# Hybrid decoder step on one core: joint level products, a readout in four quarters, and sample outer products in 32-row groups

## Chip, core and metric

The kernel runs on one core of one Trainium2 chip. The metric is the device time of one execution in microseconds (us).

## What is computed

The reference is one layer of a decoder for 256 prompt tokens and 8 sample tokens (each sample token belongs to a sequence of its own, with a stored state). The layer has two token mixers of eight heads each, a gated merge and a feed-forward block:

```python
proj = rms_norm(x, norm_mix) @ w_in            # q,k,v,gate (retention); query,forget,input,gate (HGRN2); merge gates
o_r, s_ret_new = retention_chunkwise(q, k, v, s_ret, log_gamma)     # state per head: 128 x 256
o_h, s_hg_new = hgrn2_chunkwise(qh, k_in, logf, i, s_hg)            # state per head: 128 x 128
#   for one sample token:  S = decay * S + k^T v ;  o = S^T q
x = x + (sigmoid(ga) * (o_r @ w_ret_out) + sigmoid(gb) * (o_h @ w_hgrn_out)) @ w_out
x = x + SwiGLU(rms_norm(x, norm_ffn)) ;  y = rms_norm(x, norm_final)
```

All inputs and outputs are fp32; the outputs include the new states of the prompt and of the eight samples.

## The kernel before

Tokens lie along the free dimension: 256 prompt columns and 8 sample columns, 264 in all (`T`). Weights are streamed from memory in chunks of 512 KB (four blocks of 128 rows by 256 columns). Each chunk passes through four engines in a fixed order: SyncE's queue (SP) loads it into `raw`; ScalarE (ACT) rounds it to fp32r into `hi` (L426); VectorE (DVE) writes the rest, `raw - hi`, into `lo` (L723); TensorE (PE) does 24 matmuls with it (`use_chunk`, L1082 to L1084: `hi` with the high part of the activations, `hi` with the low part, `lo` with the high part). Each of the three buffers is a ring of four, so an engine works at most four chunks ahead of the next.

The first stage is a loop over eight heads, 20 chunks a head: four for the HGRN2 query and forget logits, four for retention q and k, four for v, four for the HGRN2 input and gate, four for the retention gate. All engines run their own hand-written program in order. Between the chunks stands the work of the mixers: after chunk i of a head PE calls `tail(i)`, which finishes the head before, and `attend(i)`, which works on this head; ACT and DVE have the matching steps in the same places, after the chunk that they prepare four ahead. PSUM has two pairs of banks for the chunks (`pA`, `pB`) and four banks for the mixers: `p4`, `p56` (two banks) and `p7`. Counters such as `p4_full` and `p4_free` hand each bank from PE to its reader and back, in a numbered order of uses per head (`SC0`, `OR1`, ...).

The steps that the change touches:

- `tail(0)`: PE turns the 16 x 384 readout `o16` of the last head to columns (L1124, L1126); DVE adds the two parts of each sample.
- `attend(11)` and `attend(13)`: transposes of keys and values for both prompt blocks (L1103), and of the samples' keys and values (`rows_of`, L1107), which DVE had split into a high and a low fp32r part (L774, L776). DVE then spreads the keys over eight masked copies (`k_only`, L799).
- `attend(14)` and `attend(15)`: the outer products k^T v of the samples, four samples at a time, each a 32-row matmul (L1113) into both banks of `p56`; DVE adds each four to the decayed state `S_ret` (L905). Beside them the prompt's new state (L1164) and the prompt's outputs (L1170, L1172).
- `attend(16)`: within-block scores of HGRN2 by seven levels. GpSimd (POOL) prepares for each level a masked key `k_lev` and a query `q_lev` (L668 to L691). PE multiplies them for prompt block 0 (L1194) and for block 1 (L1196), seven matmuls each, into overlapping places of `p56`; DVE picks what it needs with seven predicated copies (L934), after a product with the identity (L917) and copies (L920, L924).
- `attend(17)`: eight outer products of the samples for HGRN2 (L1203); DVE updates `S_hg` (L941).
- `attend(19)`: the readout o = S^T q of all samples. ACT and DVE first split both new states into fp32r parts (L524, L532, L544, L809). For each sample PE multiplies both parts with a weight of 16 columns, in which only this sample's query (two parts) is not zero (`q_only`, `hq_only`, L793), and adds all up in 16 rows of `p7` (L1224).

The state of a head is loaded on SP between the chunks 13 and 14 (L371, L373), once the last head's has been written back (ACT's queue, L552, L554).

Of the kernel before, what the change touches and what calls it, by code (L numbers as in the profile page):

```python
# [41 lines left out]
P = 128  # L42
# [5 lines left out]
H = 8  # L48
# [39 lines left out]
K_IDENT = K_LEVEL + NLEV * 64  # L88
K_KDEC = K_IDENT + P
K_GAMMA = K_KDEC + 2 * H  # L90
K_EYE8 = K_GAMMA + H
K_ROW8 = K_EYE8 + NS * NS
K_SIZE = K_ROW8 + NS
# [13 lines left out]
def build(nc, consts, vectors, xT, w_in, w_ret, w_hg, w_out, w_fin, w_fout, s_ret, s_hg,  # L107
          yT, ret_p, hg_p, ret_s, hg_s):
    with ExitStack() as ctx:
# [35 lines left out]
        lb_tmp = alloc(heads, "lb_tmp", [P, 4, H])  # L145
        norm_tmp = ExitStack()
# [5 lines left out]
        hkey = alloc(heads, "hkey", [P, T])  # L152
        hquery = alloc(heads, "hquery", [P, T])
# [9 lines left out]
        v_rows = alloc(heads, "v_rows", [8 * NS, RV], F32R)  # L163
# [3 lines left out]
        key_pair = alloc(heads, "key_pair", [P, 2, 4, NS], F32R)  # L167
        k_parts, hk_parts = key_pair[:, 0], key_pair[:, 1]
        v_parts = alloc(heads, "v_parts", [P, 3, 4, NS], F32R)
        k_only = alloc(heads, "k_only", [8 * NS, NS, DK], F32R)  # L170
        q_parts = alloc(heads, "q_parts", [P, NS, 2], F32R)
        hq_parts = alloc(heads, "hq_parts", [P, NS, 2], F32R)

        q_only = alloc(heads, "q_only", [P, NS, 2, NS], F32R)
        hq_only = alloc(heads, "hq_only", [P, NS, 2, NS], F32R)
        o16 = alloc(heads, "o16", [2 * NS, 384])
# [8 lines left out]
        k_lev = [alloc(heads, f"k_lev{i}", [P, NP]) for i in range(NLEV)]  # L185
# [17 lines left out]
        S_ret_hi = alloc(heads, "S_ret_hi", [P, NS, RV], F32R)  # L203
        S_ret_lo = alloc(heads, "S_ret_lo", [P, NS, RV], F32R)
        S_hg_hi = alloc(heads, "S_hg_hi", [P, NS, HV], F32R)
        S_hg_lo = alloc(heads, "S_hg_lo", [P, NS, HV], F32R)
# [32 lines left out]
        c_level = cst[:, K_LEVEL:K_LEVEL + NLEV * 64].bitcast(I32).rearrange("p (l j) -> p l j", l=NLEV)  # L239
        c_kdec = cst[:, K_KDEC:K_KDEC + 2 * H].rearrange("p (b h) -> p b h", b=2)  # L240
        c_eye8 = cst[:, K_EYE8:K_EYE8 + NS * NS].rearrange("p (b j) -> p b j", b=NS)
        c_row8 = cst[0:8 * NS, K_ROW8:K_ROW8 + NS]
# [40 lines left out]
        hg_sig_done = sem("hg_sig_done")  # L283
        products = sem("products")
# [6 lines left out]
        state_hi = sem("state_hi")  # L291
        state_split = sem("state_split")
# [120 lines left out]
        def _(act):  # L413
# [46 lines left out]
            def tail(i, h):  # L460

                if i == 0:
                    act.wait_ge(sample_outputs, h * 2)
                    fn(o_sq[:, 0:2, :], oT[:], ACT.Square).then_inc(outputs_squared, 1)
                    fn(o_sq[:, 2, :], ohT[:], ACT.Square).then_inc(outputs_squared, 1)
                elif i == 2:
                    act.wait_ge(p56_full, h * N56 + (SS5 + 1 - N56))
                    fn(o_inv[:, 0, :], p56[:, 0, 0:T], ACT.Sqrt, bias=epsilon[:], scale=1.0 / RV)
                    fn(o_inv[:, 1, :], p56[:, 1, 0:T], ACT.Sqrt, bias=epsilon[:], scale=1.0 / HV
                       ).then_inc(p56_free, 1)  # L470

            def head(h, first=False):
# [3 lines left out]
                for i in range(HEAD_CHUNKS):  # L476
# [25 lines left out]
                    elif i == 13:  # L502
# [3 lines left out]
                        copy(v_rows[0:4 * NS], p56[0:4 * NS, 1, 0:256]).then_inc(p56_free, 1)  # L506
                    elif i == 14:

                        act.wait_ge(p7_full, h * N7 + (SF1 + 1))
                        act.wait_ge(prompt_out_ret, h * 16 + 16)  # L510
                        copy(ret_stage[:], p7[:, 0, 0:RV]).then_inc(p7_free, 1)
                        act.wait_ge(p7_free, h * N7 + (SF1 + 2))
                        act.dma_start(ret_p[bass.ds(h, 1)].rearrange("h d e -> (h d) e"), ret_stage[:]
                                      ).then_inc(prompt_out_ret, 16)
                    elif i == 15:

                        act.wait_ge(b_free, h * 2 + 3)
                        fn(hg_sig[:], hig[:, 1, :], ACT.Sigmoid).then_inc(hg_sig_done, 1)

                        act.wait_ge(normed, h * 4 + 4)  # L520
                        act.wait_ge(p4_full, h * N4 + (OR1 + 1))
                        copy(oT[:, :, 0:NP], p4[:, 0, :].rearrange("p (e n) -> p e n", e=2)).then_inc(p4_free, 1)
                        act.wait_ge(p56_free, h * N56 + (OUT1 + 2))
                        copy(S_ret_hi[:, 0:4, :], S_ret[:, 0:4, :]).then_inc(state_hi, 1)  # L524
                    elif i == 16:

                        act.wait_ge(p7_full, h * N7 + (TI2 + 1))
# [3 lines left out]
                        act.wait_ge(p56_free, h * N56 + (OUT1 + 3))  # L531
                        copy(S_ret_hi[:, 4:8, :], S_ret[:, 4:8, :]).then_inc(state_hi, 1)  # L532
                    elif i == 18:

                        act.wait_ge(p4_full, h * N4 + (OH3 + 1))
# [3 lines left out]
                        act.wait_ge(p4_free, h * N4 + (OH3 + 2))  # L539
# [3 lines left out]
                        act.wait_ge(p56_free, h * N56 + (OUTH4 + 2))  # L543
                        copy(S_hg_hi[:], S_hg[:]).then_inc(state_hi, 1)  # L544
                    elif i == 19:
# [4 lines left out]

                        act.wait_ge(state_split, h * 3 + 3)
# [4 lines left out]

                        act.wait_ge(p7_full, h * N7 + (RD3 + 1))
                        copy(o16[:], p7[0:2 * NS, 0, 0:384]).then_inc(p7_free, 1)
# [65 lines left out]
        def _(pool):  # L624
            tt = nc.gpsimd.tensor_tensor
            pool.sem_inc(normed, 4)

# [15 lines left out]
            for i in range(NLEV):  # L643
                nc.gpsimd.memset(k_lev[i][:], 0.0).then_inc(products, 1)

            steps = 2 + 4 * NLEV + 4
# [10 lines left out]
            def levels(h):  # L657

                count = [NLEV]
# [13 lines left out]
                for i in range(NLEV):  # L673
# [6 lines left out]
                    shape = [P, NP // (2 * s), s]  # L680
# [3 lines left out]
                    step(tt(kl0, k0, g0, ALU.mult))  # L684
# [6 lines left out]
                step(tt(kbar, hkey[:, 0:NP], run_g[:], ALU.mult))  # L691
                assert count[0] == NLEV + steps
# [22 lines left out]
        def _(dve):  # L715
# [56 lines left out]
            def parts(hi_out, lo_out, x, h, n):  # L772

                nc.vector.tensor_copy(hi_out, x).then_inc(parts_done, 1)  # L774
                dve.wait_ge(parts_done, h * 14 + (2 * n + 1))
                tt(lo_out, x, hi_out.bitcast(F32), ALU.subtract).then_inc(parts_done, 1)  # L776

            def twice(x):
                return x.rearrange("p (a b) -> p a b", a=1).broadcast_to([P, 2, NS])

            def key_parts(out, x, h, n):
                parts(out[:, 0:2, :], out[:, 2:4, :], twice(x), h, n)

            def value_parts(out, x, h, n):
                parts(out[:, 0:4:2, :], out[:, 1:4:2, :], twice(x), h, n)

            def query_parts(out, x, h, n):
                parts(out[:, :, 0], out[:, :, 1], x, h, n)

            def masked_query(out, q):  # L790

                shape = [P, NS, 2, NS]
                tt(out, q.bitcast(F32).rearrange("p b (c a) -> p b c a", a=1).broadcast_to(shape),  # L793
                   c_eye8.rearrange("p b (a j) -> p b a j", a=1).broadcast_to(shape), ALU.mult).then_inc(masked, 1)

            def masked_keys(out, rows64):

                shape = [8 * NS, NS, DK]
                return tt(out, rows64.rearrange("p (a d) -> p a d", a=1).broadcast_to(shape),  # L799
                          c_row8.rearrange("p (b a) -> p b a", a=1).broadcast_to(shape), ALU.mult  # L800
                          ).then_inc(masked, 1)

            def level_psum(n):

                return bass.AP(tensor=p56, offset=64 * n, ap=[[2 * 512, P], [512 + 64, 2], [1, 64]])

# [576 lines left out]
```

## Time and profile before

| | us |
|---|---|
| median of 3 runs (lowest, highest) | 1834.14 (1831.59, 1836.6) |
| the profiled execution, its own time | 1834.16 |
| span of its trace, first to last instruction | 1832.3 |
| granted TensorE clock, share of full | 0.995 |

The page of the profile gives the busy share of each engine, then the span in 40 equal slices. The first fourteen slices are the loop over the heads. TensorE is at nine tenths or more from the second slice on. VectorE is at seven or eight tenths in the loop and at five to six after it. The 16 DMA engines are at five to seven tenths, 182 GB/s on average. In the trace's lines a matmul's own duration reaches from its start to the modelled end of its pipeline, so matmuls overlap; the time that one costs is read from start to start.

### The profile page before, as it was taken

Reading aid. Unit: us, or ns where it says so; the run is one execution under the profiler, and the core shown is the slowest. Engines: PE = TensorE matmul, PEld = TensorE weight load, DVE = VectorE, ACT = ScalarE, POOL = GpSimd, SP = SyncE. Lnnn points to the kernel's source line nnn. Section 1 sums busy time; section 2 is a strip of 40 time slices with the busy share of each in tenths; the row PEclk is TensorE's granted clock in tenths of the full one; section 3 lists DMA queues with packets and bytes.
Section 4 is the critical chain, followed back from the end, with each engine's and each line's share of the span. In section 5 each row is a group of like instructions: output and inputs, shape, how many; then the busy total and the mean of one; then the engine's idle time right before and its main releaser. Section 6 shows DMA issues by size and latency. Waiting matters only on the chain.

```text
span 1832.3 us, 37809 instructions
## 1 busy us (share of the span) xinstructions
PE 1785.3 (97%) x14672; PEld 1766.0 (96%) x14672; DVE 1147.5 (63%) x1293; ACT 776.9 (42%) x894; POOL 277.4 (15%) x332
## 2 busy tenths in 40 slices
PE   5999999999999999999999999999999999999997
PEld 5999999999999999999999999999999999999996
DVE  8776877778777675555556665555555555545444
ACT  5454544445444454344444444444444444333332
POOL 4442614416144110000000000000000000000001
PEclk9999999999999999999999999999999999999998
DMA  7665646666466555555547665555565565555552
GB/s 230 192 202 177 197 139 197 190 183 196 140 193 191 184 163 185 184 183 183 182 153 245 192 183 183 182 180 181 181 182 182 183 182 182 185 184 177 179 182 102
DMA packets 388538, 333.86 MB, mean 182 GB/s; under 512 B 11776, under 2 KB 386560, under 8 KB 388352
## 3 DMA queue, kind: packets, MB, share of 16 engines
q1 hardware_dynamic: 369536, 318.88, 56.3%
q10 hardware_dynamic: 18944, 14.16, 2.5%
q8 instruction: 43, 0.70, 0.2%
q14 instruction: 15, 0.12, 0.0%
HBM read 316.67 MB, written 16.32 MB: 182 GB/s over the span
## 4 chain that ended last, share of the span: by engine, by line
PE 82%; DVE 7%; issue 4%; DMA 3%; SPq 2%; ACT 1%; DVEq 0%; POOL 0%; ACTq 0%
PE pA L1082 13%; PE pA L1084 12%; PE pA L1083 12%; PE pB L1082 10%; PE pB L1084 10%; PE pB L1083 10%; PE p L1082 3%; PE p L1084 3%; PE p L1083 3%; DMA raw<-in_w_in 2%; DVE lo L723 2%; PE p L1224 1%; SPq L348 1%; DVE hg_scores L934 1%; SPq L373 1%
## 5 line engine op out<-in xcount | busy, mean ns | idle before, releaser
L723 DVE TENSOR_TENSOR lo<-raw,hi 128x1024 fp32r<-128x1024 f32 x568 | 723.6, 1279 | 557.2 <-ACT hi L426 549.0
L426 ACT CAST hi<-raw 128x1024 fp32r<-128x1024 f32 x568 | 595.2, 1048 | 826.9 <-PE pA L1084 347.2
L1082 PE MATMUL pA<-h_hi,hi 128*128 128x264 f32 x1728 | 499.8, 289 | 19.0 <-DVE lo L723 18.7
L1083 PE MATMUL pA<-h_lo,hi 128*128 128x264 f32 x1728 | 492.0, 285 | 0.0
L1084 PE MATMUL pA<-h_hi,lo 128*128 128x264 f32 x1728 | 491.9, 285 | 0.0
L1082 PE MATMUL pB<-h_hi,hi 128*128 128x264 f32 x1472 | 421.6, 286 | 0.0
L1083 PE MATMUL pB<-h_lo,hi 128*128 128x264 f32 x1472 | 417.2, 283 | 0.0
L1084 PE MATMUL pB<-h_hi,lo 128*128 128x264 f32 x1472 | 417.2, 283 | 0.0
L1082 PEld LDWEIGHTS pA<-h_hi,hi 128*128 128x128 f32 x1728 | 327.7, 190 | 22.6 <-issue 18.9
L1083 PEld LDWEIGHTS pA<-h_lo,hi 128*128 128x128 f32 x1728 | 327.8, 190 | 0.3
L1084 PEld LDWEIGHTS pA<-h_hi,lo 128*128 128x128 f32 x1728 | 327.6, 190 | 0.0
L1082 PEld LDWEIGHTS pB<-h_hi,hi 128*128 128x128 f32 x1472 | 277.3, 188 | 0.3
L1083 PEld LDWEIGHTS pB<-h_lo,hi 128*128 128x128 f32 x1472 | 277.4, 188 | 0.2
L1084 PEld LDWEIGHTS pB<-h_hi,lo 128*128 128x128 f32 x1472 | 277.2, 188 | 0.0
L703 POOL TENSOR_TENSOR x<-x,vec 128x528 f32<-128x528 f32 x8 | 12.2, 1524 | 1151.2 <-DVE sq L1058 1151.2
L1082 PE MATMUL pA<-hid_hi,hi 128*128 128x264 f32 x352 | 99.9, 284 | 2.3 <-issue 2.3
L1082 PE MATMUL pB<-hid_hi,hi 128*128 128x264 f32 x352 | 100.3, 285 | 0.0
L1083 PE MATMUL pB<-hid_lo,hi 128*128 128x264 f32 x352 | 100.1, 284 | 0.0
L1084 PE MATMUL pB<-hid_hi,lo 128*128 128x264 f32 x352 | 100.1, 284 | 0.0
L1083 PE MATMUL pA<-hid_lo,hi 128*128 128x264 f32 x352 | 99.7, 283 | 0.0
L1084 PE MATMUL pA<-hid_hi,lo 128*128 128x264 f32 x352 | 99.5, 283 | 0.0
L1082 PE MATMUL p<-ro_hi,hi 128*128 128x264 f32 x256 | 72.7, 284 | 1.2 <-DVE ro_lo L979 1.2
(250 smaller groups left out, 2483.6 us busy)
## 6 DMA issues: line engine op xcount, KB each, us to landing
raw<-in_w_fin SPq DMA_DIRECT2D x176, 512.0 KB, 3.7
raw<-in_w_in SPq DMA_DIRECT2D x128, 512.0 KB, 3.5
raw<-in_w_in SPq DMA_DIRECT2D x192, 256.0 KB, 3.9
raw<-in_w_fout SPq DMA_DIRECT2D x88, 512.0 KB, 3.5
raw<-in_w_ret SPq DMA_DIRECT2D x32, 512.0 KB, 4.3
raw<-in_w_out SPq DMA_DIRECT2D x32, 512.0 KB, 4.2
S_ret<-in_s_ret SPq DMA_DIRECT2D x8, 1024.0 KB, 8.4
out_ret_s<-S_ret ACTq DMA_DIRECT2D x8, 1024.0 KB, 7.0
```

Source lines behind the costliest of these rows:

```text
L348: sp.dma_start(raw[s][:, :, 0:128], half(i, first, col, 0)).then_inc(raw_full[s], 16)
L373: sp.dma_start(S_hg[:], s_hg[:, bass.ds(h, 1), :, :].rearrange("b h d e -> d (b h) e")).then_inc(state_in_hg, 16)
L426: copy(hi[s], raw[s]).then_inc(hi_done, 1)
L703: tt(x2[:, 2 * g:2 * g + 2, :], x2[:, 2 * g:2 * g + 2, :], vec[:, V_FINAL + 2 * g:V_FINAL + 2 * g + 2].rearrange("p (k a) -> p k a", a=1). ...
L723: tt(lo[s], raw[s], hi[s].bitcast(F32), ALU.subtract).then_inc(split_done, 1)
L934: last = nc.vector.copy_predicated(dst, msk, src)
L1082: mm(outs[t][:, ::-1], w_hi, a_hi[:, kt, ::-1], start=(kt == 0), stop=False)
L1083: mm(outs[t][:, ::-1], w_hi, a_lo[:, kt, ::-1], start=False, stop=False)
L1084: last = mm(outs[t][:, ::-1], w_lo, a_hi[:, kt, ::-1], start=False, stop=(kt == CK * n - 1))
L1224: last = mm(p7[0:2 * NS, 0, cols], query[:, b].rearrange("p c j -> p (c j)"), part[:, b, :], start=(b == 0 and n == 0), stop=(b == NS - 1 ...
```

## The change

Four parts, each with what belongs to it:

- **Joint levels.** `k_lev` holds the keys of block 0 in its even halves and those of block 1, in reversed order, in the other halves. One matmul per level gives both blocks. POOL writes each `k_lev` with two instructions of half the size; block 1's keys, values and `kbar` are kept reversed (`hkey_back` on DVE, `hval_back` on ACT), and masks and identity are constants of twice the size.
- **Readout in four quarters.** The states are no longer split. Weight and state are fp32; each sample has a weight of 32 columns with its query in the first; four samples go to four 32-column groups of the array (`tile_position=(0, 32 * g)`), into four 32-row strips of `p7`. `o_rows` has 128 rows and `tail(0)` turns it with three full transposes. The queries need no parts: DVE copies them into place (`place_queries`) in buffers that POOL clears once.
- **Outer products in 32-row groups.** Keys and values of the samples lie four times below each other (`rows_of` gives 128 rows), masked so that each group of 32 rows holds one sample. Four matmuls, one per row group (`tile_position=(32 * g, 0)`), write four banks: `p4`, both of `p56`, and `p7`. All eight samples are done in `attend(14)`, and in `attend(17)` for HGRN2. L1164's work moves to `attend(15)`.
- **Order.** DVE updates `S_ret` in one step of the program, in four instructions of 512 columns, bank by bank; ACT's copies for the prompt state move one step later; the write-back of the states waits for the readout's copy.

```diff
-SC0, OR1, R2, OH3, TO4, N4 = 0, 1, 2, 3, 4, 5
-TV0, OUT1, L3, OUTH4, SS5, N56 = 0, 1, 3, 4, 5, 6
-TK0, SF1, TI2, RD3, N7 = 0, 1, 2, 3, 4
+SC0, OUT1, OR2, R3, OUTH4, OH5, TO6, N4 = 0, 1, 2, 3, 4, 5, 6, 7
+TV0, OUT1, L2, OUTH3, SS4, N56 = 0, 1, 2, 3, 4, 5
+TK0, OUT1, SF2, TI3, OUTH4, RD5, N7 = 0, 1, 2, 3, 4, 5, 6
...
 # scalar
-                        copy(v_rows[0:4 * NS], p56[0:4 * NS, 1, 0:256]).then_inc(p56_free, 1)
+                        copy(v_rows[:], p56[:, 1, 0:256]).then_inc(p56_free, 1)
...
+                        copy(hval_back[:], hig[:, 0, P:NP][:, ::-1]).then_inc(hval_turned, 1)
...
-                        copy(S_ret_hi[:, 0:4, :], S_ret[:, 0:4, :]).then_inc(state_hi, 1)
...
-                        copy(S_ret_hi[:, 4:8, :], S_ret[:, 4:8, :]).then_inc(state_hi, 1)
...
-                        copy(S_hg_hi[:], S_hg[:]).then_inc(state_hi, 1)
...
-                        act.wait_ge(state_split, h * 3 + 3)
+                        act.wait_ge(p7_full, h * N7 + (RD5 + 1))
+                        copy(o_rows[:], p7[:, 0, 0:384]).then_inc(p7_free, 1)
+                        act.wait_ge(p56_free, h * N56 + (OUTH3 + 2))
...
 # gpsimd
-                    step(tt(kl0, k0, g0, ALU.mult))
+                    tt(kl0, k0[:, 0:n], g0[:, 0:n], ALU.mult).then_inc(products, 1)
+                    count[0] += 1
+                    step(tt(kl1, k0[:, n:], g0[:, n:], ALU.mult))
...
-                step(tt(kbar, hkey[:, 0:NP], run_g[:], ALU.mult))
+                tt(kbar[:, 0:P], hkey[:, 0:P], run_g[:, 0:P], ALU.mult).then_inc(products, 1)
+                count[0] += 1
+                step(tt(kbar[:, P:NP][:, ::-1], hkey[:, P:NP], run_g[:, P:NP], ALU.mult))
...
 # vector
+            def place_queries(out, q):
+
+                return nc.vector.tensor_copy(
+                    out[:, :, 0:128].rearrange("p r (g j) -> p r g j", g=4)[:, :, :, 0],
+                    q.rearrange("p (r g) -> p r g", r=2)).then_inc(queries_placed, 1)
...
+                        ts(hkey_back[:], z_nsig[:, P:NP][:, ::-1], omlb[:, bass.ds(h, 1)], None, ALU.mult)
...
-                        query_parts(hq_parts, hquery[:, NP:T], h, 1)
-                        dve.wait_ge(parts_done, h * 14 + 4)
-                        masked_query(hq_only[:], hq_parts[:])
...
+                        place_queries(hq_only, hquery[:, NP:T])
...
-                        masked_keys(k_only[:], p7[0:8 * NS, 0, 256:384])
+                        masked_keys(k_only[:], p7[:, 0, 256:512].rearrange("p (c d) -> p c d", c=2))
...
+                        for g in (0, 3, 1, 2):
+                            bank, free = ((p4, p4_free), (p56, None), (p56, p56_free), (p7, p7_free))[g]
...
+                            last = stt(of_group[:, g], of_group[:, g], cst[:, bass.ds(h + K_GAMMA, 1)],
+                                       bank[:, g - 1 if g in (1, 2) else 0, :].rearrange("p (r e) -> p r e", r=2),
+                                       ALU.mult, ALU.add)
...
-                            state_lo(S_ret_lo[:, 0:4, :], S_ret[:, 0:4, :], S_ret_hi[:, 0:4, :], h, 0)
...
-                        state_lo(S_ret_lo[:, 4:8, :], S_ret[:, 4:8, :], S_ret_hi[:, 4:8, :], h, 1)
...
-                        state_lo(S_hg_lo[:], S_hg[:], S_hg_hi[:], h, 2)
...
 # tensor
+            def sample_updates(keys, values, width):
+
+                banks = (p4[:, 0], p56[:, 0], p56[:, 1], p7[:, 0])
+                for r in range(2):
+                    for g in range(4):
+                        rows = slice(32 * g, 32 * g + 32)
+                        last = mm(banks[g][:, r * width:r * width + width], keys[rows, r, :], values[rows, :],
+                                  start=True, stop=True, tile_position=(32 * g, 0))
+                        if r == 1 and g != 1:
+                            last.then_inc((p4_full, None, p56_full, p7_full)[g], 1)
...
-                    mm(p4[:, 0, 0:16], o16[:, 0:128], one16, start=True, stop=True)
-                    for e in range(1, 3):
-                        last = transpose(p4[:, 0, 16 * e:16 * e + 16], o16[:, e * 128:e * 128 + 128], one16)
+                    for e in range(3):
+                        last = transpose(p4[:, 0, e * P:e * P + P], o_rows[:, e * P:e * P + P], c_ident)
...
-                    rows_of(p7[0:8 * NS, 0, 256:384], key_pair[:]).then_inc(p7_full, 1)
+                    rows_of(p7[:, 0, 256:384], k_parts)
+                    rows_of(p7[:, 0, 384:512], hk_parts).then_inc(p7_full, 1)
...
                     pe.wait_ge(keys_copied, h + 1)
+                    pe.wait_ge(p4_free, h * N4 + (OUT1 + 1))
+                    pe.wait_ge(p7_free, h * N7 + (OUT1 + 1))
                     pe.wait_ge(p56_free, h * N56 + (OUT1 + 1))
-                    sample_updates(0, h)
...
+                    pe.wait_ge(masked, h + 1)
+                    sample_updates(k_only[:, 0], v_rows, RV)
...
                     for n in range(NLEV):
-                        mm(p56[:, 0, 64 * n:64 * n + P], k_lev[n][:, 0:P], q_lev[n][:], start=True, stop=True)
-                    for n in reversed(range(NLEV)):
-                        last = mm(p56[:, 1, 64 * n:64 * n + P], k_lev[n][:, P:NP], q_lev[n][:], start=True, stop=True)
+                        last = mm(p56[:, n // 4, (n % 4) * P:(n % 4) * P + P], k_lev[n][:], q_lev[n][:],
+                                  start=True, stop=True)
...
+                    pe.wait_ge(p4_free, h * N4 + (OUTH4 + 1))
+                    pe.wait_ge(p7_free, h * N7 + (OUTH4 + 1))
+                    pe.wait_ge(p56_free, h * N56 + (OUTH3 + 1))
+                    sample_updates(k_only[:, 1], hv_rows, HV)
...
-                    pe.wait_ge(p56_free, h * N56 + (L3 + 2))
-                    pe.wait_ge(p7_free, h * N7 + (TI2 + 2))
+                    pe.wait_ge(p4_free, h * N4 + (OH5 + 1))
...
+                    pe.wait_ge(queries_placed, h * 2 + 2)
+                    pe.wait_ge(p7_free, h * N7 + (RD5 + 1))
+                    pe.wait_ge(p56_free, h * N56 + (OUTH3 + 2))
+                    for query, state, cols in ((q_only, S_ret, slice(0, RV)), (hq_only, S_hg, slice(RV, 384))):
+                        rows = query[:].rearrange("p r x -> p (r x)")
+                        for r in range(2):
+                            for g in range(4):
+                                b = 4 * r + g
+                                last = mm(p7[32 * g:32 * g + 32, 0, cols], rows[:, 32 * b:32 * b + 32], state[:, b, :],
+                                          start=(r == 0), stop=(r == 1), tile_position=(0, 32 * g))
```

## Rows read from the trace of the kernel before

**Rows 1.** The page, part 1: busy us of each engine, share, instructions.
```profile
PE 1785.3 (97%) x14672; PEld 1766.0 (96%) x14672; DVE 1147.5 (63%) x1293; ACT 776.9 (42%) x894; POOL 277.4 (15%) x332
```

**Rows 2.** Waits of PE: line, releaser: us in total, times, longest us.
```profile
PE p L1103 <- DVE v_parts L776: 8.2, 6, 1.6
```

**Rows 3.** Timeline of PE, third head: start us, us, line, out<-in, shapes, count.
```profile
212.54 0.28 PE L1084 MATMUL pB<-h_hi,lo 128*128 128x264 f32 x1
212.66 0.59 PE L1147 MATMUL p<-qk 128*128 128x256 f32 x2
213.09 0.38 PE L1148 MATMUL p<-qk 128*128 128x128 f32 x2
```

**Rows 4.** Timeline of PE around `tail(0)`, then around `attend(11)`.
```profile
175.71 0.28 PE L1084 MATMUL pA<-h_hi,lo 128*128 128x264 f32 x1
...
176.60 0.28 PE L1083 MATMUL pA<-h_lo,hi 128*128 128x264 f32 x1
...
209.32 0.28 PE L1084 MATMUL pA<-h_hi,lo 128*128 128x264 f32 x1
...
209.90 0.28 PE L1083 MATMUL pB<-h_lo,hi 128*128 128x264 f32 x1
```

**Rows 5.** Timeline of PE around `attend(14)`.
```profile
221.43 0.28 PE L1084 MATMUL pB<-h_hi,lo 128*128 128x264 f32 x1
221.64 0.74 PE L1113 MATMUL p<-v_rows,k_only 32*128 32x256 f32 x4
222.31 1.13 PE L1164 MATMUL p<-v_nat,kd_nat 128*128 128x256 f32 x4
...
223.40 0.28 PE L1083 MATMUL pB<-h_lo,hi 128*128 128x264 f32 x1
```

**Rows 6.** Timeline of PE in `attend(16)`: the two runs of levels.
```profile
232.43 1.73 PE L1194 MATMUL p<-q_lev,k_lev 128*128 128x128 f32 x14
233.99 1.73 PE L1196 MATMUL p<-q_lev,k_lev 128*128 128x128 f32 x14
```

**Rows 7.** Timeline of PE around `attend(17)`; in brackets the idle time before.
```profile
238.34 0.28 PE L1084 MATMUL pA<-h_hi,lo 128*128 128x264 f32 x1
238.85 1.10 PE L1203 MATMUL p<-v_rows,k_only 32*128 32x128 f32 x8 [0.23 <-DVE hg_scores L934]
239.88 0.39 PE L1082 MATMUL pA<-h_hi,hi 128*128 128x264 f32 x1
```

**Rows 8.** Timeline of PE in `attend(19)`: first of each state, then the next chunk.
```profile
246.89 0.28 PE L1224 MATMUL p<-S_ret_hi,q_only 128*16 128x256 f32 x1
...
248.77 0.22 PE L1224 MATMUL p<-S_hg_hi,hq_only 128*16 128x128 f32 x1
...
249.73 0.33 PE L1082 MATMUL pA<-h_hi,hi 128*128 128x264 f32 x1
```

**Rows 9.** Chain that ended last, third head: start us, us, what.
```profile
195.19 0.68 DVE hq_parts L774
...
196.53 2.69 DVE lo L723 x2
...
206.44 5.82 DMA raw<-in_w_in
```

**Rows 10.** Timeline of DVE in the same head, steps 16 and 17.
```profile
234.08 0.28 DVE L920 CAST v_rows<-p 32x128 fp32r<-32x128 f32 x1
235.76 0.29 DVE L924 COPY hg_scores<-p 128x128 f32<-128x128 f32 x1 [1.39 <-PE p L1196]
235.96 2.83 DVE L934 COPY_PREDICATED hg_scores<-cst,p 128x128 f32<-128x128 int32 x7
...
240.88 2.15 DVE L941 SCALAR_TENSOR_TENSOR S_hg<-S_hg,forget,p 128x128 f32<-128x128 f32 x8
```

**Rows 11.** The tile `k_lev` on POOL: durations in ns min/median/max, first and last start.
```profile
L684 POOL TENSOR_TENSOR k_lev<-hkey,run_g x56: 448/462/1509, 42.2 to 598.7; 128x128 f32<-128x128 f32 x56
```

**Rows 12.** Timeline of POOL: its last instruction in the third head.
```profile
219.54 1.60 POOL L691 TENSOR_TENSOR rg_sig<-hkey,run_g 128x256 f32<-128x256 f32 x1
```

More of the change, by code:

```diff
@@ L152, in build @@
         hkey = alloc(heads, "hkey", [P, T])
+        hkey_back = alloc(heads, "hkey_back", [P, P])
+        hval_back = alloc(heads, "hval_back", [P, P])
         hquery = alloc(heads, "hquery", [P, T])
@@ L184, in build @@
         S_hg = alloc(heads, "S_hg", [P, NS, HV])
-        k_lev = [alloc(heads, f"k_lev{i}", [P, NP]) for i in range(NLEV)]
+        k_lev = [alloc(heads, f"k_lev{i}", [P, P]) for i in range(NLEV)]
         run_f = alloc(heads, "run_f", [P, NP])
@@ L202, in build @@
         passing.close()
[L203 to L206, printed above, removed]
         heads.close()
@@ L642, in _ @@
             pool.wait_ge(h_done, 4)
-            for i in range(NLEV):
-                nc.gpsimd.memset(k_lev[i][:], 0.0).then_inc(products, 1)
-            steps = 2 + 4 * NLEV + 4
+            steps = 2 + 5 * NLEV + 5
             def last_outputs(h):
@@ L781, in key_parts @@
             def key_parts(out, x, h, n):
-                parts(out[:, 0:2, :], out[:, 2:4, :], twice(x), h, n)
+                parts(out[:, :, 0:2, :], out[:, :, 2:4, :], twice(x), h, n)
             def value_parts(out, x, h, n):
[L785 to L800, printed above, removed]
+                parts(out[:, :, 0:4:2, :], out[:, :, 1:4:2, :], twice(x), h, n)
+            def place_queries(out, q):
+                return nc.vector.tensor_copy(
+                    out[:, :, 0:128].rearrange("p r (g j) -> p r g j", g=4)[:, :, :, 0],
+                    q.rearrange("p (r g) -> p r g", r=2)).then_inc(queries_placed, 1)
@@ L1096, in _, with natural @@
                 pe.sem_inc(free, 1)
-            steps = 2 + 4 * NLEV + 4
-            def natural(out, src, width):
+            steps = 2 + 5 * NLEV + 5
+            def natural(out, src, width, second=None):
                 for b in range(2):
-                    last = transpose(out[:, b * width:b * width + 128], src[:, b * P:b * P + P], c_ident)
+                    block = src[:, b * P:b * P + P] if second is None or b == 0 else second
+                    last = transpose(out[:, b * width:b * width + 128], block, c_ident)
@@ L1104, in natural @@
                 return last
             def rows_of(out, parts):
-                return transpose(out, parts.rearrange("p a q b -> p (a q b)").bitcast(F32), c_ident)
-            def sample_updates(q, h):
-                pe.wait_ge(masked, h * 3 + 3)
-                for b in range(4):
-                    last = mm(p56[:, b // 2, (b % 2) * 256:(b % 2) * 256 + 256], k_only[0:4 * NS, 4 * q + b, :],
-                              v_rows[0:4 * NS, :], start=True, stop=True)
-                last.then_inc(p56_full, 1)
+                return transpose(out, parts.rearrange("p g q b -> p (g q b)").bitcast(F32), c_ident)
@@ L1174, in attend @@
                     last.then_inc(p4_full, 1)
-                    pe.wait_ge(p56_free, h * N56 + (OUT1 + 2))
-                    sample_updates(1, h)
+                    pe.wait_ge(p7_free, h * N7 + (SF2 + 1))
+                    for b in range(2):
+                        last = mm(p7[:, 0, 0:RV], kd_nat[:, b, :], v_nat[:, b, :], start=(b == 0), stop=(b == 1))
+                    last.then_inc(p7_full, 1)
                 elif i == 16:
-                    pe.wait_ge(products, h * steps + (NLEV + steps))
@@ L1180, in attend @@
-                    pe.wait_ge(p7_free, h * N7 + (TI2 + 1))
-                    pe.wait_ge(parts_done, h * 14 + 14)
-                    natural(p7[:, 0, 0:256], hig[:, 0, :], 128)
+                    pe.wait_ge(products, h * steps + steps)
+                    pe.wait_ge(p7_free, h * N7 + (TI3 + 1))
+                    pe.wait_ge(parts_done, h * 10 + 10)
+                    pe.wait_ge(hval_turned, h + 1)
+                    natural(p7[:, 0, 0:256], hig[:, 0, :], 128, second=hval_back[:])
@@ L1202, in attend @@
-                    for b in range(NS):
-                        last = mm(p56[:, b // 4, (b % 4) * 128:(b % 4) * 128 + 128], k_only[4 * NS:8 * NS, b, :],
-                                  v_rows[4 * NS:8 * NS, 0:HV], start=True, stop=True)
-                    last.then_inc(p56_full, 1)
+                    pe.wait_ge(p4_free, h * N4 + (OUTH4 + 1))
+                    pe.wait_ge(p7_free, h * N7 + (OUTH4 + 1))
+                    pe.wait_ge(p56_free, h * N56 + (OUTH3 + 1))
+                    sample_updates(k_only[:, 1], hv_rows, HV)
```

216 lines of the change are left out of this document (101 added, 115 removed).

## The prediction, written before the changed kernel had run

> **What bounds the kernel now.** I read the page first: TensorE is busy for 97% of the span [rows 1]. A busy TensorE can still be waiting inside, so the list of its waits comes next. There is one that matters in the loop over the heads: `attend(13)` stood for the samples' value parts in six heads of eight, 8.2 us in all [rows 2]. Third is PE's own timeline, read from start to start. Between two chunks the 24 matmuls of a chunk follow each other at 0.12 us (212.54 to 212.66) [rows 3], and each piece of mixer work pushes the next chunk back by its whole length. So a head is 480 such matmuls, 57.6 us, plus the mixer pieces one after another, and the change is priced as the sum of what each piece loses or gains on PE. Work taken from VectorE, ScalarE or the queues counts only where a PE wait ends on it. Fourth is the chain of waits, for the one place where it leaves PE: from `tail(2)` it runs over DVE, SP's queue and a weight load to `attend(13)`.
>
> I take an extra piece as the distance from the last matmul of one chunk to the second of the next, less 0.24 us for two regular steps.
>
> **Part by part, per head, then times eight.**
>
> *Levels.* Fourteen fp32 records, which are seven matmuls (each fp32 matmul shows as two records), run from 232.43 to 233.99: 1.56 us, 0.223 a matmul [rows 6]. The second run of seven goes: -1.56, -12.5 us in all. Part comes back at `attend(17)`, which waits for DVE's predicated copies. The seven copies (L934) end at 238.79; the last chunk ends at 238.34 + 0.12 and PE goes on at 238.85 [rows 7, 10]. Afterwards `p56` is full 1.56 us earlier, but DVE's L924 can come forward only from 235.76 to the end of L920 at 234.36, by 1.40 [rows 10]. So PE's gap grows by 0.16: +1.3 in all. The reversed copies on ACT and DVE are small; ACT loses three copies of whole states in exchange, and nobody on PE waits for it.
>
> *POOL.* It gets eight more instructions a head. Nearest is L684 at 0.45 to 1.51 us, for twice the columns [rows 11]. At the median 0.46 that is 3.7 us, at the maximum 12.1. POOL now ends at 221.14 [rows 12], the levels start at 232.43 less about 1.2 us for what stands in front (five transposes at 0.11, three matmuls at 0.22), and the pieces before them get about 1.6 us shorter. That leaves 8.5 us, so I take 0; beyond 1.06 us an instruction PE would wait, up to 3.6 us a head. I take the median, because the halves are smaller.
>
> *Small transposes.* `tail(0)` now costs 176.60 - 175.71 - 0.24 = 0.65; three full transposes cost 0.34 at `attend(11)` (209.90 - 209.32 - 0.24) [rows 4]. The change makes `tail(0)` three full ones: -0.31, -2.5 in all. `attend(11)` gets a fourth: +0.11, +0.9 in all. `attend(13)` keeps four.
>
> *Outer products, retention.* Four 32-row matmuls take 221.64 to 222.31: 0.67, 0.167 each. With the idle step before them (221.43 + 0.12 to 221.64, 0.09) and a slow step behind, about 0.11, four cost 0.87 [rows 5]; there are two such fours, 1.73 together. Streaming 256 columns takes about 0.11: the readout with 16-column weights does one every 0.117 (1.88 us for 16) and one of 128 columns every 0.06 [rows 8]. So some 0.06 of the 0.167 is the weight load, which isn't hidden when consecutive matmuls use the same 32 rows. After the change consecutive ones use other rows and banks. Bounds for eight: everything overlaps, two rounds of 0.167, 0.33; nothing overlaps, 1.34. I take loads one after the other and the matmuls under them, 8 x 0.06 + 0.11 = 0.6, because in the chunks too loads go one by one under matmuls. With one entry and exit, 0.20, that is 0.80 in place of 1.73: -0.93, -7.4 in all (ends -9.6 and -1.5). L1164 moves to `attend(15)` at the same price. The new waits for `p4` and `p7` have behind them all of PE's stream: `p4` needs DVE's score product of step 12 first, which DVE reaches no later, since the key mask in front of it halves; at `attend(15)` it needs one quarter of the `S_ret` update, 512 columns, at most 1.1 us by L941's 0.27 for 128 [rows 10], under a chunk of 2.88. Cost 0; at most 1 us a head if DVE is late.
>
> The Trainium skill, "TensorE: Matmul & The Clock Gate", section on packing small matmuls, gives 3.07 times for four row tiles. By it eight would take about 0.44 and the sum would be some 1.3 us lower; no run here shows it yet.
>
> *Outer products, HGRN2.* Eight take 1.03 (238.85 to 239.88) [rows 7], 0.129 each, so about 0.07 is load. By the same reasoning 8 x 0.074 + 0.055 = 0.65: -0.38, -3.0 in all (ends 0.26 and 1.03: -6.2 and 0). What follows is later on DVE: `attend(18)` now needs the first two of eight `S_hg` steps (L941, from 240.88, 2.03 after L1203 began; two take 0.54) and comes 3.6 us after; `attend(19)` needs all, 4.2 after, and comes more than a chunk (2.88) after `attend(18)` [rows 7, 10]. Cost 0.
>
> *Readout.* It takes 249.73 - 246.89 = 2.84 now, with a slow first step of the next chunk 2.9 [rows 8]. The change makes it 16 fp32 matmuls. An fp32 matmul of 256 columns takes 0.43 (212.66 to 213.09) as two records, 0.215 a pass [rows 3]; one of 128 columns 0.11 a pass. All one after another is 16 x 0.215 + 16 x 0.11 = 5.2; four at once is a quarter, 1.3. The trace of before has no column groups, so these are the bounds. I take the middle one: records start in the order of the program in every timeline here, and the second pass of a matmul needs the columns that its first pass occupies. So it can't start before the first ends, and the next quarter's first pass, standing behind it, can only run beside it. Two passes run at any time: 8 x 0.215 + 8 x 0.11 + 0.11 = 2.7, with entry and exit 2.9. Gain 0.
>
> *The wait at `attend(13)`.* DVE's query parts and masking between 195.19 and 196.53 go, 1.34 us; they stand on the chain before the loads of `lo`, behind which SP starts the next weights, the state and the weights that land from 206.44 on [rows 9]. What comes in (a reversed key copy, two small placements, key parts four times as wide) I put at 0.75 by the neighbours in the chain. So the wait ends about 0.6 earlier, PE gets there 0.11 later in relation, and the wider value parts give some back: -0.45 in six heads, -2.7 in all; ends 0 and all 8.2.
>
> Write-back of the states now waits for the readout's copy, a microsecond or so later than now; the next head's load needs it only after twelve chunks. The larger constants delay SP's queue once, at the start, where four chunks are already there. Both 0.
>
> **Sum:** -12.5 + 1.3 - 2.5 + 0.9 - 7.4 - 3.0 + 0 - 2.7 = -25.9. The profiled execution's own time is 1834.16, equal to the median 1834.14: 1808.
>
> **Rivals.**
> 1. *Four quarters at once.* If the passes of one quarter don't hold up the next, the readout takes 1.3 + 0.2: -1.4 a head, 1797. For it: matmuls on other columns share nothing. Against: program order of the starts.
> 2. *The readout runs one at a time* while the row groups overlap: 5.2 + 0.2 is +2.5 a head, 1828. The same page of the Trainium skill says that weight loads are pulled under running matmuls only for other row groups, which column tiles don't have; the chunks' loads here do run under matmuls of all rows [rows 3], which speaks against it.
> 3. *Slower: tiled matmuls don't overlap at all.* L1113 shows that a matmul on 32 rows waits for its own load and for its predecessor. If this holds across groups, the outer products gain only one entry (1.5 us in all, HGRN2 nothing): 1837.6 with the serial readout; each of its 32 loads then shows, from 0.01 (16-column weights) to 0.06 (128): 1840 to 1853. It decides from a readout of 5.0 us on. "TensorEngine Tiling (Array Packing)" of the Trainium skill, key properties, says that a change of tiling mode drains the array, which would add to this.
> 4. *POOL's levels come late*, up to 3.6 us a head: up to 1837.
> 5. *A new wait* on DVE at `attend(14)`, `(15)` or `(17)` takes back one us a head: 1816.
>
> **Numbers.** Chances: forecast 0.42, rival 1 0.25, rival 2 0.13, rival 3 0.10, rival 4 0.04, rival 5 0.06. About 0.3%, 5.5 us, is what a measurement of this kernel can tell from no change. Faster by more: the forecast, rivals 1 and 5, half of 2, half of 4, 0.82. Within: half of 2, half of 4, a little of 3, 0.10. Slower: 0.08. With the ends of the outer products and of the wait at `attend(13)` the forecast's own range is 1798 to 1820. Rivals 1 and 2 widen it to 1794 to 1830; what is left out is most of 3 and 4 and the low end of 1.
>
> **What would show it.** Right: L1194's successor with 14 records in 1.56 us and no second run; `attend(17)` waiting about 0.4 us for the predicated copies; the eight outer products within 0.6 us; the readout near 2.9 us with its records starting 0.2 apart; the wait at `attend(13)` still there in most heads. Wrong: readout records starting within 0.05 us of each other (rival 1) or above 5 us in all (2, 3); L1113's successors still 0.167 apart; a wait of PE for POOL.

## The result and the profile after

The changed kernel takes 1793.76 us (median of 4 runs, 1790.38 to 1794.92) against 1834.34: the ratio is 0.9776, with a 95% interval of 0.9757 to 0.9796. The profiled execution took 1792.81, its span is 1791.0. The forecast was 1808 with a range from 1794 to 1830, so the sign was right, the gain, 40.6 us, was half as large again as the 26 forecast, and the time lies 0.24 us below the lower end of the range. It is near that of rival 1 (four quarters at once), which stood at 1797 with a chance of 0.25.

The page, part 1, and the list of PE's waits (line, releaser: us in total, times, longest us), to be read beside [rows 1, 2]:

```profile
PE 1746.1 (97%) x14560; PEld 1729.1 (97%) x14560; DVE 1099.7 (61%) x1261; ACT 752.2 (42%) x878; POOL 298.9 (17%) x391
...
PE p L1090 <- DVE v_parts L765: 5.1, 7, 1.8
PE p L1102 <- DVE hg_scores L917: 3.2, 8, 0.6
```

TensorE is as full as before and is busy for 39 us less. The wait at `attend(13)` is still there, 5.1 us in place of 8.2.

The timeline of PE in one head, piece by piece (start us, us, line, out<-in, shapes, count). `tail(0)`, as in [rows 4]:

```profile
239.59 0.28 PE L1070 MATMUL pA<-h_hi,lo 128*128 128x264 f32 x1
239.71 0.49 PE L1114 MATMUL p<-cst,o_rows 128*128 128x128 f32 x3
...
240.16 0.28 PE L1069 MATMUL pA<-h_lo,hi 128*128 128x264 f32 x1
```

The outer products of retention, as in [rows 5], and the levels, as in [rows 6]:

```profile
283.94 0.28 PE L1070 MATMUL pB<-h_hi,lo 128*128 128x264 f32 x1
284.15 0.51 PE L1102 MATMUL p<-v_rows,k_only 32*128 32x256 f32 x8
284.58 0.39 PE L1068 MATMUL pB<-h_hi,hi 128*128 128x264 f32 x1
284.81 0.29 PE L1069 MATMUL pB<-h_lo,hi 128*128 128x264 f32 x1
...
293.96 1.73 PE L1185 MATMUL p<-q_lev,k_lev 128*128 128x128 f32 x14
295.45 0.37 PE L1068 MATMUL pA<-h_hi,hi 128*128 128x264 f32 x1
```

The outer products of HGRN2, as in [rows 7], and the readout, as in [rows 8]:

```profile
298.32 0.28 PE L1070 MATMUL pA<-h_hi,lo 128*128 128x264 f32 x1
298.98 0.44 PE L1102 MATMUL p<-hv_rows,k_only 32*128 32x128 f32 x8 [0.37 <-DVE hg_scores L917]
299.35 0.39 PE L1068 MATMUL pA<-h_hi,hi 128*128 128x264 f32 x1
299.57 0.28 PE L1069 MATMUL pA<-h_lo,hi 128*128 128x264 f32 x1
...
306.23 0.28 PE L1070 MATMUL pA<-h_hi,lo 128*128 128x264 f32 x1
306.44 1.07 PE L1212 MATMUL p<-S_ret,q_only 128*32 128x256 f32 x16
307.33 0.62 PE L1212 MATMUL p<-S_hg,hq_only 128*32 128x128 f32 x16
307.88 0.39 PE L1068 MATMUL pA<-h_hi,hi 128*128 128x264 f32 x1
308.11 0.28 PE L1069 MATMUL pA<-h_lo,hi 128*128 128x264 f32 x1
```

Eight outer products now take 0.43 us (284.15 to 284.58) and 0.37 (298.98 to 299.35), where four took 0.67 and eight 1.03. The sixteen readout matmuls take 1.44 (306.44 to 307.88), where the old ones took 2.84. They are 32 records in the trace, two passes for each fp32 matmul. One after another these passes would need 5.2, so they run about four abreast. Two narrower windows of the same timeline (its first 0.06 and its first 0.31 us) show how they start:

```profile
306.44 0.42 PE L1212 MATMUL p<-S_ret,q_only 128*32 128x256 f32 x4
...
306.44 0.64 PE L1212 MATMUL p<-S_ret,q_only 128*32 128x256 f32 x8
```

Four records start within the first 0.06 us and the next four some 0.2 later. The forecast had records starting 0.2 apart, with two passes running at any time.

### The profile page after: what moved, and what is told of

It is laid out like the page before. It is cut to its first block, busy times and chain, and to the rows that moved or that the text cites. A ratio compares the mean times of both kernels' runs of the same rounds, so it can differ in the third digit from the quotient of the medians.

```text
span 1791.0 us, 37605 instructions
## 1 busy us (share of the span) xinstructions
PE 1746.1 (97%) x14560; PEld 1729.1 (97%) x14560; DVE 1099.7 (61%) x1261; ACT 752.2 (42%) x878; POOL 298.9 (17%) x391
## 4 chain that ended last, share of the span: by engine, by line
PE 81%; DVE 7%; issue 4%; DMA 3%; SPq 2%; ACT 2%; DVEq 0%; POOL 0%; ACTq 0%
PE pA L1068 13%; PE pA L1070 12%; PE pA L1069 12%; PE pB L1068 11%; PE pB L1070 11%; PE pB L1069 11%; PE p L1068 3%; PE p L1070 3%; PE p L1069 3%; DMA raw<-in_w_in 2%; DVE lo L712 2%; SPq L343 1%; ACT hi L421 1%; DVE hg_scores L917 1%; PE p L1212 1%
```

## Experiments

Each kernel is the changed one with one edit, unless it says otherwise; e7 has the edits of e5 and e6. All times are medians; the kernel before took 1833.9 to 1835.0 on the same chips.

| kernel | us | ratio to the kernel before, 95% interval |
|---|---|---|
| e1_one_quarter | 1823.67 | 0.9925 to 0.9958 |
| e10_two_quarters | 1803.64 | 0.9821 to 0.9854 |
| e2_order | 1793.15 | 0.9757 to 0.9790 |
| e3_one_row_group | 1803.84 | 0.9815 to 0.9847 |
| e4_levels_twice | 1803.45 | 0.9815 to 0.9848 |
| e8_splits_back | 1797.28 | 0.9783 to 0.9809 |
| e9_before_state_later (kernel before, edited) | 1824.26 | 0.9932 to 0.9966 |
| e5_state_later | 1786.87 | 0.9725 to 0.9751 |
| e6_back_late | 1791.15 | 0.9752 to 0.9779 |
| e7_both | 1786.10 | 0.9723 to 0.9750 |

### e1_one_quarter: the readout in one column group

```diff
-                                last = mm(p7[32 * g:32 * g + 32, 0, cols], rows[:, 32 * b:32 * b + 32], state[:, b, :],
-                                          start=(r == 0), stop=(r == 1), tile_position=(0, 32 * g))
+                                last = mm(p7[0:32, 0, cols], rows[:, 32 * b:32 * b + 32], state[:, b, :],
+                                          start=(b == 0), stop=(b == NS - 1), tile_position=(0, 0))
```

> All sixteen readout matmuls of a head go to the first 32 columns of the array and add up in one strip of p7 (so the eight samples' outputs are mixed; nothing else changes). Theory: the four column groups work side by side, and that is where most of the gain beyond the forecast came from. Then the passes now stand in one line: 16 x 0.215 + 16 x 0.11 + 0.2 = 5.4 us a head in place of 1.65, +3.75 a head, +30 in all: 1824. Rival: the readout became short because it has half as many matmuls and weights of 32 columns, and the groups don't matter: 1.65 stays, 1794.

PE's timeline of its readout:

```profile
242.06 3.64 PE L1212 MATMUL p<-S_ret,q_only 128*32 128x256 f32 x16
245.54 1.91 PE L1212 MATMUL p<-S_hg,hq_only 128*32 128x128 f32 x16
247.38 0.39 PE L1068 MATMUL pA<-h_hi,hi 128*128 128x264 f32 x1
```

The same 32 records take 5.32 us in one group, and the kernel 1823.67, as expected. The column groups alone are worth 30 us here: with the readout in one line, the change as a whole would have gained 11.

### e10_two_quarters: the readout in two column groups

```diff
-                                last = mm(p7[32 * g:32 * g + 32, 0, cols], rows[:, 32 * b:32 * b + 32], state[:, b, :],
-                                          start=(r == 0), stop=(r == 1), tile_position=(0, 32 * g))
+                                k = g % 2
+                                last = mm(p7[32 * k:32 * k + 32, 0, cols], rows[:, 32 * b:32 * b + 32], state[:, b, :],
+                                          start=(b < 2), stop=(b >= NS - 2), tile_position=(0, 32 * k))
```

> The readout uses two column groups instead of four, eight matmuls in each (so outputs of samples are mixed; nothing else changes). Theory: the readout's time is the passes of the fullest group, whatever their number: 8 x 2 passes in each, half of 5.2, with entry and exit 2.8 a head in place of 1.65: +9, 1802. Rival: four groups side by side are already held back by something they share, and two at once cost less than twice: below 1799.

Its readout on PE's timeline:

```profile
308.41 1.92 PE L1213 MATMUL p<-S_ret,q_only 128*32 128x256 f32 x16
310.17 1.04 PE L1213 MATMUL p<-S_hg,hq_only 128*32 128x128 f32 x16
311.14 0.39 PE L1068 MATMUL pA<-h_hi,hi 128*128 128x264 f32 x1
```

It takes 2.73 us and the kernel 1803.64. One, two and four groups take 5.32, 2.73 and 1.44: the time is that of the passes in the fullest group, plus some 0.1. Nothing that the groups share held them back. Two abreast is also what the forecast had assumed for four groups (2.7), so this run shows what the kernel would have done had that assumption held.

### e2_order: both matmuls of a group directly after each other

```diff
-                for r in range(2):
-                    for g in range(4):
+                for g in range(4):
+                    for r in range(2):
                         rows = slice(32 * g, 32 * g + 32)
...
-                        for r in range(2):
-                            for g in range(4):
+                        for g in range(4):
+                            for r in range(2):
                                 b = 4 * r + g
                                 last = mm(p7[32 * g:32 * g + 32, 0, cols], rows[:, 32 * b:32 * b + 32], state[:, b, :],
```

> Same work; only the order in which matmuls are written changes: both matmuls of one group directly after each other, in the readout and in the outer products. Theory of the forecast (starts follow the program, so a second matmul that needs busy columns or rows holds up all that stand behind it): in the readout each group then delays the next by three passes, 4 x 0.645 + 0.215 = 2.8 for retention and 1.4 for HGRN2, 4.4 with entry and exit in place of 1.65, and the outer products grow from 0.64 to about 1.0 and by 0.3 for HGRN2: +3.4 a head, 1821. Rival: each group has a line of its own and passes overtake those of other groups: nothing changes, 1794.

PE's timeline of a readout, and of the start of another in a window of its first 0.06 us:

```profile
305.70 1.09 PE L1212 MATMUL p<-S_ret,q_only 128*32 128x256 f32 x16
306.59 0.66 PE L1212 MATMUL p<-S_hg,hq_only 128*32 128x128 f32 x16
307.18 0.39 PE L1068 MATMUL pA<-h_hi,hi 128*128 128x264 f32 x1
...
92.77 0.44 PE L1212 MATMUL p<-S_ret,q_only 128*32 128x256 f32 x4
```

Nothing changed: 1.48 us, four records at the start, 1793.15; the outer products, rewritten in the same way, cost 0.65 us a piece in place of 0.63 or 0.64. In the text of this kernel three passes of group 0 stand between its first and the first pass of group 1, and still four records start together. So a pass that waits for its own columns doesn't hold up those of other groups written behind it. This refutes the step on which the forecast of the readout rested. The records don't name their group, so which pass overtakes which isn't read from the trace; that the four starts belong to four groups follows from e1, where one group starts one at a time.

### e3_one_row_group: all outer products on the first 32 rows

```diff
-                        rows = slice(32 * g, 32 * g + 32)
+                        rows = slice(0, 32)
                         last = mm(banks[g][:, r * width:r * width + width], keys[rows, r, :], values[rows, :],
-                                  start=True, stop=True, tile_position=(32 * g, 0))
+                                  start=True, stop=True, tile_position=(0, 0))
```

> The eight outer products of each kind all use the first 32 rows, and still write the same four banks (so the new states of most samples get another sample's product). Theory: the row groups overlap loads and matmuls, nothing else does; on one group each costs 0.167 and 0.129 as in the kernel before: 8 x 0.167 + 0.2 = 1.54 in place of 0.64 and 8 x 0.129 + 0.63 = 1.66 in place of 1.01, +1.55 a head, 1806. Rival: it is the change of PSUM bank from one matmul to the next that lets them overlap: 1794.

PE's timeline of the retention ones:

```profile
287.65 1.21 PE L1102 MATMUL p<-v_rows,k_only 32*128 32x256 f32 x8
288.79 0.39 PE L1068 MATMUL pB<-h_hi,hi 128*128 128x264 f32 x1
```

Eight take 1.14 us on one row group, 0.43 on four; the kernel takes 1803.84, 10 more than the changed one (12 expected). It is the row groups that overlap, not the banks: the banks still alternate here. The weight loads of these matmuls show the difference. The first line is from the kernel before, the second from e3, the last two from the changed kernel, and the last of all is a window that holds only its first 0.05 us:

```profile
221.64 0.54 PEld L1113 LDWEIGHTS p<-v_rows,k_only 32*128 32x128 f32 x4
...
287.65 1.01 PEld L1102 LDWEIGHTS p<-v_rows,k_only 32*128 32x128 f32 x8
...
284.15 0.30 PEld L1102 LDWEIGHTS p<-v_rows,k_only 32*128 32x128 f32 x8
...
284.15 0.19 PEld L1102 LDWEIGHTS p<-v_rows,k_only 32*128 32x128 f32 x4
```

One such load lasts 0.18 us in the trace. On one row group the loads start (1.01 - 0.18) / 7 = 0.12 us apart, and so they do in the kernel before: (0.54 - 0.18) / 3 = 0.12. On four row groups four of them start within 0.01. So the 0.167 a matmul that the prediction read from [rows 5] is 0.12 from start to start, with a longer first and last step spread over four matmuls; eight of them take 1.14, not 1.34.

### e4_levels_twice: the level matmuls done twice

```diff
-                    for n in range(NLEV):
+                    for n in list(range(NLEV)) * 2:
```

> The seven level matmuls are done twice with the same operands; the result is the same. Theory: levels are paid in full on TensorE and the predicated copies of VectorE give back a little: +1.56 a head, and the gap ahead of the next outer products shrinks by about 0.16, so +1.4 a head, +11: 1805. Rival: VectorE or GpSimd sets the time of this stage by now: 1794 to 1797.

It takes 1803.45, 9.7 more; 11 were expected. The levels are paid on TensorE (`attend(16)` grows from 2.79 to 4.34 us a head), and the predicated copies behind them give back a little: the wait for `hg_scores` falls from 3.2 to 2.0 us, as the list of waits of this kernel says:

```profile
PE p L1102 <- DVE hg_scores L917: 2.0, 8, 0.3
```

### e8_splits_back: the splitting of the states put back, unused

```diff
+                        copy(S_ret_hi[:, 0:4, :], S_ret[:, 0:4, :]).then_inc(state_hi, 1)
...
+                        copy(S_ret_hi[:, 4:8, :], S_ret[:, 4:8, :]).then_inc(state_hi, 1)
...
+                        copy(S_hg_hi[:], S_hg[:]).then_inc(state_hi, 1)
...
+                        act.wait_ge(state_split, h * 3 + 3)
...
+                        state_lo(S_ret_lo[:], S_ret[:, 0:4, :], S_ret_hi[:, 0:4, :], h, 0)
...
+                        state_lo(S_ret_lo[:], S_ret[:, 4:8, :], S_ret_hi[:, 4:8, :], h, 1)
...
+                        state_lo(S_hg_lo[:], S_hg[:], S_hg_hi[:], h, 2)
```

> The changed kernel with the splitting of the new states put back as work without use: three casts on ScalarE and three subtractions on VectorE a head, in the places that they had, and the write-back of the states waiting for them; the readout still reads the unsplit states. Theory: what the change took off these two engines in the second half of a head was hidden, and the gain is TensorE's: 1793, and no new wait of PE above 0.3 us. Rival: the lighter VectorE brings part of the gain: up to 3.7 us a head, 1800 to 1820.

Neither: 1797.28, 3.5 us more than the changed kernel. The intervals of the two ratios overlap a little, so the waits have to say where it goes. Its list of PE's waits:

```profile
PE p L1121 <- DVE hg_scores L934: 4.1, 8, 0.5
PE pA L1087 <- DVE rg_gate L844: 2.1, 7, 0.3
```

With the six instructions a head back, the copies at step 16 end later (4.1 in place of 3.2 us), and VectorE frees `pA` so late that the next head's first chunk waits 0.3 us in seven heads, which neither kernel showed. That is 3.0 us of longer waits. So the work that was taken off these engines is worth up to a tenth of the gain, though the kernel before shows no wait for `pA` there and only 1.9 us for `hg_scores`: in the shorter stage it is uncovered.

### e5, e6, e7 and e9: the wait at attend(13)

e5 and e9 move the state loads on SP, in the changed kernel and in the kernel before:

```diff
-                    if i == 1:
+                    if i == 3:
                         sp.wait_ge(state_out, h * 32 + 32)
                         sp.dma_start(S_ret[:], s_ret[:, bass.ds(h, 1), :, :].rearrange("b h d e -> d (b h) e")
```

> SP issues the loads of the states behind the weights of chunk 15 instead of chunk 13; nothing else changes. Theory: the wait that is left at attend(13) (5.1 us in seven heads) ends with weights that stand behind 1.5 MB of state in the DMA queues; it goes, about -5: 1788 to 1790. Rival: VectorE's own chain in front of those loads sets it: wait stays, 1793. Second rival: the state then comes too late for its update at step 14, a wait of PE at attend(15): slower, 1800.

> The kernel before with one edit: SP issues the state loads behind the weights of chunk 15 instead of chunk 13. Theory: the state loads cause the wait at attend(13) here too (8.2 us in six heads); it goes: 1826 to 1828. Rival: in the kernel before VectorE's query parts set this wait, and the load order matters only after the change: 1834.

In both the wait is gone from the list, and `attend(13)` costs 0.66 us in every head. In the changed kernel it costs 1.1 to 2.7 in seven heads, 6.7 us more in all, and in the kernel before 2.1 to 2.4 in six heads and 1.0 in one, 9.9 more in all. The gains agree with that: e5 comes to 1786.87, 6.9 less, and the kernel before to 1824.26, 9.6 less than on the same chip without the edit. So the weights that this wait ends with are late because of the state loads in front of them, in both kernels. The chain of waits in a head of the changed kernel shows how (start us, us, what):

```profile
263.73 1.42 SPq L368
265.40 3.35 SPq L343
268.93 6.06 DMA raw<-in_w_in
```

Behind the state loads (L368 is the second of them) SP takes 3.35 us to issue the next weights, where its four weight issues just before took 0.37 each, and the chain then stands 6.06 for the transfer, where loads of this size take 3.8 in the median. How much of the delay is SP's and how much the transfer's wasn't tried apart.

The chain of waits in a head of e5 no longer leaves PE; its longest pieces (start us, us, what) between one readout and `attend(12)` are:

```profile
302.32 1.44 PE p L1212 x32
303.76 0.32 PE pA L1068
306.87 0.33 PE p L1114 x3
312.97 0.45 PE p L1121 x2
313.42 0.45 PE p L1122 x2
343.15 0.43 PE p L1136 x2
```

e6 takes the reversed key copy out of the chain that leads there:

```diff
-                        ts(hkey_back[:], z_nsig[:, P:NP][:, ::-1], omlb[:, bass.ds(h, 1)], None, ALU.mult)
...
+                    elif i == 9:
+
+                        ts(hkey_back[:], z_nsig[:, P:NP][:, ::-1], omlb[:, bass.ds(h, 1)], None, ALU.mult)
```

> VectorE's reversed copy of the keys (hkey_back) is done at step 9 instead of step 3. Theory: at step 3 it takes 0.3 to 1.3 us on the chain that ends at attend(13), and the wait there gets shorter by 0.3 to 1 us in seven heads: 1787 to 1791. Rival: something else is late next in that chain: 1793.

It takes 1791.15 and its wait is 4.0 us in place of 5.1. Nothing follows from that. The intervals of the ratio overlap with the changed kernel's, and six kernels whose edits lie elsewhere (e1, e2, e3, e4, e8, e10) show 3.3 to 5.0 us for the same wait. The copy lasts 1.26 us in the changed kernel's chain, but without it VectorE's stretch from the first instruction of this step (`hqf`) to the next `lo` shrinks only from 6.67 to 6.44 us, because the instructions behind it take longer.

> Both: the state loads behind chunk 15 and the reversed copy at step 9. Theory: the wait at attend(13) is gone whole and not more than that is to be had, 1788. Rival: the two together uncover a later wait, 1793.

e7 takes 1786.10, as e5 within the noise: with the state loads out of the way, the copy makes no difference that can be measured. e5 and e7 are faster than both kernels: 0.9738 and 0.9736 of the kernel before.

## Why the prediction was right and wrong, step by step

- **What bounds it**: right. The edits that lengthened mixer pieces on TensorE lengthened the kernel by about as much: summed over the eight heads of the trace the pieces grew by 31.0 (e1), 10.9 (e3), 11.2 (e4) and 10.3 us (e10), and the time by 29.9, 10.1, 9.7 and 9.9.
- **Levels**: right. One run of 14 records remains, and `attend(16)` falls from 4.34 to 2.79 us, -12.4 in all (-12.5 forecast); e4 shows that they are paid. The gap ahead of `attend(17)` grew from 0.39 to 0.54 us (298.32 + 0.12 to 298.98), 0.16 forecast.
- **Small transposes**: right. `tail(0)` is 240.16 - 239.59 - 0.24 = 0.33 (0.34 forecast), and `attend(11)` grew by 0.11, as forecast; -1.6 in all.
- **Outer products**: direction right, size too small. I took the weight loads one after another, 0.6 and 0.65 us for eight; they measured 0.43 and 0.37, near the lower ends 0.33 and 0.26. Loads of different row groups start together (e3). The 0.06 put down for a load at 256 columns came from 0.167 less the streaming, and that 0.167 held the slow first and last step. With entry and exit, and `attend(15)` at 2.18 us in most heads in place of 2.16, the gains are 8.5 and 5.3 us in place of 7.4 and 3.0, some 3.4 us of the miss. The Trainium skill, "TensorE: Matmul & The Clock Gate", section on packing small matmuls, gives 3.07 times for four row tiles, measured with 512 columns. Here, with 256, e3 over the changed kernel is 1.14 / 0.43 = 2.7. The prediction's estimate of 0.44 by that figure came close because it divided 1.34, where e3 has 1.14.
- **Readout**: this step failed. I put it at 2.9 us, no gain; it is 308.11 - 306.23 - 0.24 = 1.64 with the slow steps around it, -1.25 a head, -10.0 us, most of the miss. The argument was that records start in the order of the program, so that the second fp32 pass of one quarter holds up the next quarter and only two passes run at any time. Four do. Every timeline of the kernel before does show starts in order, but it holds no column groups, so it couldn't decide this; I had the four-abreast case as the other bound and chose by a rule that the trace showed only for matmuls on the same columns. e2 shows that the rule doesn't hold between groups, e10 what it would have cost.
- **The wait at `attend(13)`**: right in size (-2.7 forecast, -3.1 measured) and in place: it stayed, in seven heads now. The size is in part luck: one execution of each kernel was traced, and the variants whose edits lie elsewhere show 3.3 to 5.0 us of wait, which is -3.2 to -4.9. VectorE's stretch from `hqf` to the next `lo` fell from 7.45 to 6.67 us in the third to eighth head, 0.78 where I had 0.6. No run put the query parts back, so that this is what shortened the wait isn't shown. What I missed is what the wait hangs on: with the state loads moved it is gone in both kernels (e5, e9).
- **POOL** was late nowhere (rival 4): no wait of PE for it is in the list. **Rivals 2 and 3** fell with the changed kernel's timeline; e1 and e3 show what serial tiles would have cost, 30 and 10 us. **Rival 5**: the new waits for `p4` and `p7` show in no list.
- **The range**: rival 1 with everything else as forecast is 1797, and the range ended 3 us below that. The readout and the outer products missed on the same side, and the range had room for one of them.

Added up from the traces, per run: levels -12.4, gap +1.2, transposes -1.6, outer products -8.5 and -5.3, readout -10.0, `attend(13)` -3.2, together -39.8 of the 41.3 between the two profiled executions. Of the rest 1.3 is in one place: in the third to eighth head of the kernel before, the first matmul of one chunk starts 0.34 us behind its predecessor in place of 0.12, and in the changed kernel it doesn't. What it stood for there isn't known.

## What to carry to other kernels

Where TensorE is full from start to start, price small matmuls by their distance in the timeline, and look for pieces with few rows or few columns: put in separate 32-row or 32-column groups, four of them cost little more than one here. Count the passes of the fullest group; the order in which the groups are written didn't matter here. When a bound decides the forecast and the trace has no row for it, let the range hold the near case of every open term at once.

When a wait sits behind weight loads, look at what else was put into the DMA queues just ahead: moving 1.5 MB of state two chunks later gave 7 us in the changed kernel and 10 in the one before.

## What the runs showed of the hardware that was not expected

- The sixteen fp32 matmuls of 32 columns take 5.32, 2.73 and 1.44 us on one, two and four column groups, and 1.48 on four groups with the two matmuls of a group written together.
- Eight 32-row fp32r matmuls of 256 columns take 1.14 us on one row group and 0.43 on four.
- Four weight loads of 32 x 128 start within 0.01 us of each other when they go to four row groups, and 0.12 us apart when they go to one.
